# First pair's preparation ahead of the second pair's projection; V mixed by VectorE instead of ScalarE and GpSimd

## The reference, cut to what matters

```python
def rwkv_prepare(h, mu, w_in, w0, w1, w2, a0, a1, a2, k_k, k_a):
    xx = centred_shift(h)                 # 0.5 * (previous + next token) - h
    lerp = lambda j: h + xx * mu[j]       # six mixes: r, k, v, gate, w, a
    r, k, v = (heads(lerp(j) @ w_in[j]) for j in range(3))
    gate = lerp(3) @ w_in[3]
    logw = heads(-exp(-softplus(-(w0 + tanh(lerp(4) @ w1) @ w2)) - 0.5))
    a = heads(sigmoid(a0 + (lerp(5) @ a1) @ a2))
    kk = normalised(k * k_k);  k_dir = k * (1 + (a - 1) * k_a);  b = kk * a
    return r, logw, k_dir, v, -kk, b, gate

def step(s, inp):                         # wkv_scan, once per token and direction
    r_t, lw_t, k_t, v_t, a_t, b_t = inp
    sa = einsum('dbhij,dbhj->dbhi', s, a_t)
    s = s * exp(lw_t) + sa * b_t + v_t * k_t
    return s, einsum('dbhij,dbhj->dbhi', s, r_t)
```

## Time and profile before

| what | value |
| --- | --- |
| median of 3 runs | 2491.7 us (2485.37 to 2492.45) |
| the profiled execution's own time | 2497.76 us |
| its span in the trace | 2496.1 us |
| PE busy | 2240.5 us (90% of the span) |
| DVE busy | 1001.0 us (40%) |
| ACT busy | 530.7 us (21%) |
| POOL busy | 313.6 us (13%) |
| granted TensorE clock, mean | 0.939 of full speed |

### The profile page before, as it was taken

One profiled execution on the slowest core, in us unless ns is written; L12 is line 12 of the kernel. 1 busy time (PEld: TensorE's weight loads), 2 busy tenths in 40 slices (PEclk: granted clock), 3 DMA queues, 4 the chain that ended last, 5 costly groups with the idle time before them and its releaser, 6 DMA issues. The chain is left out here.

```text
span 2496.1 us, 39647 instructions
## 1 busy us (share of the span) xinstructions
PE 2240.5 (90%) x16688; PEld 1643.2 (66%) x16688; DVE 1001.0 (40%) x2256; ACT 530.7 (21%) x939; POOL 313.6 (13%) x536
## 2 busy tenths in 40 slices
PE   2998997999999998999986799999998899879898
PEld 1887886787888776888842355556666665446556
DVE  3451633534430572776070533433433531230252
ACT  1112220311000102100022344333333322011151
POOL 0000000000000300000007533342431020000000
PEclk9998998999999999999988899998998799989989
DMA  7454336437854311676026645545443252103000
GB/s 307 175 200 153 113 137 210 93 140 283 304 230 170 132 52 62 277 302 252 34 80 251 194 125 145 144 133 122 136 131 76 56 197 86 68 5 135 34 1 17
DMA packets 127132, 359.76 MB, mean 144 GB/s; under 512 B 78696, under 2 KB 87144, under 8 KB 109424
## 3 DMA queue, kind: packets, MB, share of 16 engines
q1 hardware_dynamic: 93776, 209.90, 24.6%
q0 software_dynamic: 32608, 146.31, 17.3%
q10 hardware_dynamic: 576, 1.05, 0.1%
HBM read 340.36 MB, written 16.85 MB: 143 GB/s over the span
## 5 line engine op out<-in xcount | busy, mean ns | idle before, releaser
L271 PE MATMUL bank<-h,ring 128*128 128x256 f32 x2304 | 500.2, 380 | 4.8 <-DVEq L1074 3.3
L271 PEld LDWEIGHTS bank<-h,ring 128*128 128x128 f32 x2304 | 438.8, 191 | 68.3 <-DVEq L1074 4.9
L1927 PE MATMUL bank<-rw_feed 128*128 128x512 f32 x464 | 258.8, 667 | 27.4 <-DMA rw_feed<-in_rkvg 27.2
L185 PE MATMUL bank<-con 128*128 128x512 f32 x250 | 121.1, 634 | 77.3 <-PEq L257 57.1
L1714 POOL DMA_DIRECT2D rw_feed<-rwkv_mixes x232 | 124.8, 538 | 505.0 <-PE bank L1927 494.6
L2230 DVE TENSOR_TENSOR rw_u<-bank,rw_lam 128x128 f32<-128x128 f32 x120 | 34.9, 291 | 328.4 <-PE bank L1846 325.6
L984 PE MATMUL bank<-ffn_hidden,ring 128*128 128x256 f32 x704 | 152.4, 379 | 3.4 <-PEq L1010 3.4
L488 PE MATMUL bank<-h,ring 128*128 128x256 f32 x640 | 145.9, 386 | 8.3 <-PEq L288 8.3
L984 PEld LDWEIGHTS bank<-ffn_hidden,ring 128*128 128x128 f32 x704 | 133.6, 190 | 22.2 <-issue 4.1
L1927 PEld LDWEIGHTS bank<-rw_feed 128*128 128x128 f32 x464 | 81.3, 203 | 99.0 <-issue 53.3
L488 PEld LDWEIGHTS bank<-h,ring 128*128 128x128 f32 x640 | 122.2, 193 | 28.2 <-issue 11.9
(11 more groups left out here) (414 smaller groups left out, 3409.3 us busy)
## 6 DMA issues: line engine op xcount, KB each, us to landing
ring<-in_stream SPq DMA_DIRECT2D x79, 2048.0 KB, 8.0
rw_feed<-rwkv_mixes POOLq DMA_DIRECT2D x232, 256.0 KB, 3.0
next_w<-in_mod_stream POOLq DMA_DIRECT2D x24, 2048.0 KB, 9.4
ctx<-in_mod_rest POOLq DMA_DIRECT2D x16, 1024.0 KB, 7.0
rw_feed<-in_rkvg POOLq DMA_DIRECT2D x232, 64.0 KB, 3.3
rwkv_mixes<-mixed SPq DMA_DIRECT2D x8, 1024.0 KB, 3.9
y<-bias_table SPq DMA_DIRECT2D x48, 128.0 KB, 5.0
rw_at<-rw_at_kept SPq DMA_DIRECT2D x16, 256.0 KB, 5.3
```

The costliest lines, as they stand in the source:

```text
L185: pe.matmul(k.psum[bank][:], const(k, "ident"), k.con[:, 0:512], start=True, stop=True)
L271: mm = pe.matmul(out, ring_tile(k, n, kt, i * P), rhs[kt], start=start and kt == kts[0], stop=stop and kt == kts[-1])
L1927: pe.matmul(k.psum[PROJ], feed[:, g % FEED, 512:], feed[:, g % FEED, 0:512], start=(kt == 0), stop=(kt == KT - 1)).then_inc(eaten, 1)
```

## The change

It has two parts. In stage one the mix V is made by DVE, with the same instruction as the other mixes, behind K and R and after a wait for the first low-rank product, which reads the buffer that V takes. ACT and POOL make only G. In the list of stage two, the preparation of pair 0 is put at positions 0 to 0.4 of its round in place of 0.42 to 1; the other pairs' positions stay.

```diff
@@ stage_rwkv_in, gpsimd
-            for n, j in enumerate((V, G)):
-                for kt in range(KT):
-                    pool.wait_ge(scaled, KT * n + kt + 1)
-                    nc.gpsimd.tensor_tensor(place[j][:, kt, :], place[j][:, kt, :], h[:, kt, :], ALU.add).then_inc(
-                        mixed[j], 1)
+            for kt in range(KT):
+                pool.wait_ge(scaled, kt + 1)
+                nc.gpsimd.tensor_tensor(place[G][:, kt, :], place[G][:, kt, :], h[:, kt, :], ALU.add).then_inc(mixed[G], 1)
@@ vector
-            for j in (K, R):
+            for j in (K, R, V):
+                if j == V:
+                    dve.wait_ge(lora_up, 1)
                 for kt in range(KT):
                     mix(j, kt).then_inc(mixed[j], 1)
@@ scalar
-            for j in (V, G):
-                for kt in range(KT):
-                    nc.scalar.activation(place[j][:, kt, :], xx[:, kt, :], ACT.Copy, scale=row(k, "mu", 8 * j + kt)).then_inc(
-                        scaled, 1)
+            for kt in range(KT):
+                nc.scalar.activation(place[G][:, kt, :], xx[:, kt, :], ACT.Copy, scale=row(k, "mu", 8 * G + kt)).then_inc(
+                    scaled, 1)
@@ scan_order
-                            (0.42, 1, has(i + 3, scan_ready(i + 3))),
+                            (0.42 if i + 3 else 0, 1 if i + 3 else 0.4, has(i + 3, scan_ready(i + 3))),
```

## The result

The changed kernel took 2475.66 us in the median of 6 runs (2463.11 to 2479.05), the kernel before 2492.07 us (2485.37 to 2497.86, 6 runs). The ratio is 0.9932, with a 95% interval of 0.9909 to 0.9954: faster by 17 us, between 11 and 23. The forecast was 8.7 us. The profiled execution of the changed kernel took 2475.85 us, its span is 2474.2.

What follows compares the result with a forecast made beforehand. PE was taken as the engine to follow, with gains only where PE or a block's end waits: 4.45 us at stage one's end plus 4.3 at the scan's head made 8.7, so 2491.7 - 8.7 = 2483.0 us, range 2476 to 2490.5.

Steps and rivals of the forecast that it cites:

- Part A: End of stage one: V on DVE lets POOL's G and the last write end earlier, gaining 4.45 us.
- the row with the one long addition: Stage one: POOL's first addition took 2971 ns, others 1257; read as held up until DVE stopped, giving 4.45 us.
- Part B: Head of the scan: pair 0's preparation goes ahead of the 24 tiles; gram at +36.2 against +40.9, gain 4.3 us.
- bounds 1.7 and 5.3: Scan head: gain 1.7 us if the clock rises only after the third tile, 5.3 if PE is warm and copies hide.
- the first tiles' pace: Scan head: POOL issues tile 6 at about +12.2, then one tile each 1.06 us, so tile 23 at +30.2.
- the lower bound: Scan head: clock rises only after the third tile, tile 8 issued at +16.4, tile 23 ends at +37.9; gain 1.7 us.
- One sign that I had named for being wrong: Scan head: tile waits on `in_rkvg` that put the gram past +39.
- The step that failed: Behind the second `el`, everything stays equal, so the head's 4.3 us gain stands to the end.
- 1: Gain shrinks: six-deep feed falls behind at the scan head, or stage one gives nothing; 0 to 7.5 us gained, chance 0.30.
- 3: Low clock stays on through the scan's 24 tiles: 2499 if all are cold; chance 0.08 together with other losses.
- the three: Smaller gain (0.30); over 10.5 us, POOL not held up and PE warm, 2480.3 (0.12); low clock through tiles (0.08, with other losses).

Runs made afterwards that it cites:

- order alone: Only the list order of stage two changed, on the kernel before, with V still on ScalarE and GpSimd: 2482.95 against 2489.67 us, ratio 0.9982.
- beside the eight instructions: New order plus eight tiny VectorE instructions on the kernel before, V unmoved: ratio 0.9948, against 0.9956 for those instructions without the new order.
- The eight memsets: Eight one-column VectorE memsets added in the small block ahead of the scan, on the kernel before: 2481.99 against 2492.23 us, ratio 0.9956.
- the second: The changed kernel measured again, without further edit, against the kernel before: 2467.78 against 2489.67 us, ratio 0.9907 (0.9884 to 0.993).
- V alone: Only the mix of V moved to VectorE, list order as in the kernel before: 2470.81 against 2489.67 us, ratio 0.9916.

## Why the prediction was half right

- **Part A** (4.45 us): right, 4.5 measured, by the row with the one long addition. The Trainium skill (SBUF — State Buffer, SBUF: two separate sides) has the port pair that VectorE and GpSimd share locked for one whole instruction. The trace agrees that the addition is blocked, and goes further: it lasted 8350 ns, while DVE ran some eleven instructions. The prediction said that the rule "would give the 4.45"; a lock of one instruction does not say so much, and what gave the 4.45 was the long row.
- **Missing beside it**: 0.8 us in the small block, in every trace with V on DVE. The change leaves that block as it was, and the cause was not tested.
- **Part B** (4.3 us, bounds 1.7 and 5.3): mechanism right, size too high: 1.6 to 1.8 in the first pair of traces, 3.4 in the mean at the gram. The times say 4 us (order alone, from none to 9) and 2 us (beside the eight instructions). The mis-sized term is the first tiles' pace. POOL issued tiles 6, 7 and 8 of the changed kernel at +13.7, +15.4 and +17.0, 1.6 to 1.7 us apart, as at the low clock; I had +12.2 and 1.06. That is the case that I had kept as the lower bound, tile 8 at +16.4. Tile 23 was then issued at +33.5 instead of +30.2 and began at +38.1 instead of +34.7. One sign that I had named for being wrong was there in this trace: PE waited 1.08 and 0.43 us for `in_rkvg`, and the gram came at +39.09, past +39.
- **The step that failed** is the last one: "Behind the second `el` the items, their waits and the DMA round trips of the triangular solve are the same and relative to it, so I let the gain stand to the end." The items are the same, but DVE's program is not the same length, and I had costed its eight instructions by their busy time alone. They took away a hole 570 us later, which had held DVE up by 0.35 us, and with it 9.5 us that the low clock had cost behind it. The eight memsets gave the same tail without any of the change, and a delay of 0.35 us at that place took it away from the changed kernel. So the larger part of the gain is luck: it belongs to the layout of DVE's program and not to the idea.
- The sum by what was measured: 4.5 + 0.8 + 9.5 + 3.4 = 18.2 us, inside the interval of the first comparison (11 to 23) and just inside that of the second (17 to 29). V alone does not add up as well: it gave 21 us (16 to 26), where its terms make 14.8.
- **Rivals**: 1 did not come about, though part B sat at its low end in the first trace. 3 (a clock that stays low through the tiles) did not come about: only the first tiles were slow. None of the three named a clock that is decided elsewhere.

The hole stood in the trace before, as an "issue" row of 0.45 us. What could have been asked beforehand is where an engine waits for "issue" in the long stage, and whether the clock falls soon behind it.

What stays open is, first, why DVE stops for 0.45 us at that instruction. The stop goes away with four, eight or sixteen instructions more ahead of it, and is there in all three traces without them, each time beside a packet of the instruction queue q14. That fits a supply of instructions that depends on the place in the program, but a wait for it is not shown. Second, the runs set DVE's delay and not PE's: that PE's longer stand before the gram is what lowers the clock is read from the traces and was not tested by itself.

Open too is the middle of the scan. From the inverse of pair 2 to the bonus of pair 3 it took 42.9 to 43.8 us in eight traces and 38.9 in six. The clock tells them apart as well. From 33.5 to 43.5 us behind inverse 2, the kernel before (43.8) and V alone (38.9):
```profile
1620.79:1630.79 10.00, 8.59 (x65) 4.92 (x67) 2.58 (x4) 2.92 (x5) 0.24 (x1) 0.50 0.54 100
1609.79:1619.79 10.00, 9.52 (x140) 6.44 (x140) 2.58 (x5) 4.07 (x7) 1.70 (x4) 1.00 0.55 116
```
It is 0.50 to 0.54 in the eight and 1.00 in the six. The six share no edit that the eight lack, and the two programs that have two traces (before, changed) were long in both. Whether these 5 us change from one execution to the next, or belong to a program, is not shown.

## What to carry to other kernels

An edit that adds or drops instructions on an engine moves everything behind it in that engine's program, and can make or remove a short stop far from itself; so look in the trace before for "issue" rows on engines that PE waits for, and compare lengths between fixed instructions along the whole trace before a gain is put down to the edit. Where a stage's clock falls and rises at fixed places, a delay of some tenths of a microsecond ahead of such a place can cost over twenty times its length (0.35 us cost 9.7 here), and elsewhere only its own length (0.4 us one pair earlier, where a later stretch even came out 1.7 us shorter). Adding a few idle instructions is a cheap test of whether a gain belongs to the idea or to the layout of the program.

## What the runs showed of the hardware

- A GpSimd addition beside back-to-back DVE instructions with two SBUF inputs took 8350 ns instead of 1262 and ended 1.1 us behind DVE's last one, with DVE's own at 746. Before, the first addition did the same over a shorter rest: 2971 ns, ending 1.1 us behind DVE.
- PE standing 1.67 instead of 1.31 us before one gram, at a place where it is busy before and behind, was followed by a granted clock of 0.83, 0.89 and 0.60 in three stretches of 10 us, which begin some 5 us behind it, in place of 1.00. That was so in all four traces with such a delay and in none of the ten without. A smaller delay, about 0.06 us, left the clock up there.
- An "issue" row can be a real wait: the 1.42 us at L2230 ended 0.1 us behind PE's product. The other one, 0.45 us at L2158, had nothing that its waits ask for ending near it; what stands beside it is a packet of the instruction queue q14, in three of three traces and in none of the eleven without the hole.
